# Eight recurrent heads of one encoder layer: the head outputs made with tokens on the partitions, their squares summed along the free axis, scaled, and turned around by PE

## The reference, cut to what matters

```
o  = (q * exp(G)) @ S_before_chunk  +  tril(att) @ v          # 128 numbers per token and head
o  = o * rsqrt(mean(o * o, over the 128 numbers) + eps) * a_gnorm
o  = o * silu(og)
```

## Time and profile before

| | us |
|---|---|
| median of 3 runs | 2349.55 |
| lowest, highest | 2348.75, 2355.37 |
| span of the profiled execution | 2347.9 |
| PE busy / DVE / ACT / POOL | 2281.0 / 1565.2 / 1268.0 / 1337.0 |

### The profile page before, as it was taken

How to read it: one execution, slowest core, us unless ns; L and a number is a source line. 1 busy time by engine, 2 the same in 40 slices (tenths; PEclk the granted TensorE clock), 3 DMA queues, 4 the chain that set the end, 5 groups by cost and what they waited for, 6 DMA issues and landing times.

```text
span 2347.9 us, 54490 instructions
## 1 busy us (share of the span) xinstructions
PE 2281.0 (97%) x20432; PEld 1959.8 (83%) x20432; DVE 1565.2 (67%) x2618; ACT 1268.0 (54%) x2295; POOL 1337.0 (57%) x1019
## 2 busy tenths in 40 slices
PE   8899999999998999999999999999999999999998
PEld 6788888888887888888878888877888888888886
DVE  7877777635589777777882332389687767445755
ACT  6454555433576666666554334554555544334775
POOL 2787777767515555555555444305777778677120
PEclk9999999999999999999999999999999999999999
DMA  3123222443530111111111212330232222535202
GB/s 132 50 83 101 92 77 86 151 143 103 166 100 20 40 46 46 44 39 41 49 43 49 63 48 86 115 101 28 86 92 89 86 77 86 178 122 194 76 19 75
DMA packets 155236, 194.93 MB, mean 83 GB/s; under 512 B 13168, under 2 KB 102512, under 8 KB 155120
## 3 DMA queue, kind: packets, MB, share of 16 engines
q1 hardware_dynamic: 111920, 153.59, 20.7%
q10 hardware_dynamic: 43200, 39.83, 5.2%
HBM read 155.49 MB, written 37.88 MB: 82 GB/s over the span
## 4 chain that ended last, share of the span: by engine, by line
PE 65%; DVE 13%; POOL 7%; issue 6%; ACT 5%; DMA 3%; SPq 1%; ACTq 0%; POOLq 0%; DVEq 0%
PE bank L1068 17%; PE bank L1071 17%; PE bank L1070 17%; PE bank L1035 4%; PE bank L1037 4%; PE bank L1036 4%; POOL ring L929 4%; DMA ring<-weights 3%; POOL ring L933 2%; DVE hid L2201 2%; DVE hid L2355 1%; DVE ops L2256 1%; DVE ops L2365 1%; DVE ops L2209 1%; PE bank L1201 1%
## 5 line engine op out<-in xcount | busy, mean ns | idle before, releaser
L1068 PE MATMUL bank<-ops,ring 128*128 128x264 f16 x4112 | 1139.4, 277 | 20.2 <-DVE work L2402 6.3
L1070 PE MATMUL bank<-ops,ring 128*128 128x264 f16 x4112 | 1138.7, 277 | 0.0
L1071 PE MATMUL bank<-ops,ring 128*128 128x264 f16 x4112 | 1138.6, 277 | 0.0
L929 POOL TENSOR_TENSOR ring<-ring 128x512 f16<-128x512 f32 (+1 forms) x492 | 659.8, 1360 | 273.8 <-ACT ring L1401 273.8
L1401 ACT ACTIVATE ring<-ring 128x512 f16<-128x512 f32 (+1 forms) x492 | 286.7, 614 | 501.8 <-POOL ring L933 498.3
L1068 PEld LDWEIGHTS bank<-ops,ring 128*128 128x128 f16 x4112 | 404.4, 98 | 91.3 <-issue 9.8
L1071 PEld LDWEIGHTS bank<-ops,ring 128*128 128x128 f16 x4112 | 403.7, 98 | 61.7
L1070 PEld LDWEIGHTS bank<-ops,ring 128*128 128x128 f16 x4112 | 403.7, 98 | 60.3
L914 POOL TENSOR_TENSOR ring<-wtmp,ring 128x512 f16<-128x512 f32 x107 | 130.8, 1227 | 340.9 <-ACT ring L1342 340.3
L1035 PE MATMUL bank<-hid,ring 128*128 128x264 f16 x1068 | 294.9, 276 | 1.5 <-issue 1.3
L1037 PE MATMUL bank<-hid,ring 128*128 128x264 f16 x1068 | 294.8, 276 | 0.0
(11 more groups left out here) (227 smaller groups left out, 3626.5 us busy)
## 6 DMA issues: line engine op xcount, KB each, us to landing
ring<-weights SPq DMA_DIRECT2D x363, 256.0 KB, 2.7
ops<-spill SPq DMA_DIRECT2D x16, 1056.0 KB, 6.9
ring<-weights SPq DMA_DIRECT2D x120, 128.0 KB, 2.4
spill<-hid ACTq DMA_DIRECT2D x42, 264.0 KB, 2.9
spill<-hid ACTq DMA_DIRECT2D x20, 528.0 KB, 5.0
ops<-spill SPq DMA_DIRECT2D x8, 792.0 KB, 5.1
hid<-xT SPq DMA_DIRECT2D x8, 528.0 KB, 8.3
hid<-out_x ACTq DMA_DIRECT2D x8, 528.0 KB, 7.3
```

The costliest lines, as they stand in the source:

```text
L929: nc.gpsimd.tensor_tensor(low(slot, kh), weight_source(name, k, kh), high(slot, kh), ALU.subtract)\
L1068: nc.tensor.matmul(out, whi, xhi, start=(kk == 0 and fresh(name, k)), stop=False, skip_group_check=True)
L1070: nc.tensor.matmul(out, whi, xlo, start=False, stop=False, skip_group_check=True)
L1071: mm = nc.tensor.matmul(out, wlo, xhi, start=False, stop=end, skip_group_check=True)
```

## The change

`head_outputs` swaps the operands: att or the decayed q (`W[5]`) is now the stationary side, v or the state `Sn` streams, and the output has tokens on partitions. `head_sumsq` goes. ACT squares the pieces (four of 256 columns and one of 64x128), DVE sums them with `tensor_reduce` into `osum` [128 x 9]. At the next turn ACT does Ln and Exp on `osum` (`orstd`), ahead of `logf`, and after `logf` copies the nine output tiles out of PSUM, each with its per-partition scale (`orows`). PE turns the nine tiles around (`output_transposes`, pieces OT), and DVE multiplies them, out of PSUM, with a_gnorm and silu(og) (`onorm`, which is now three instructions). The head loop of PE is written out for h = 1 and h = 8.

```diff
 HG_PIECES = (["vT"] * 3 + ["kT"] * 3 + ["L32"] * 2 + ["L16"] * 2 + ["D16"] * 2
-             + ["P"] * 5 + ["O"] * 4 + ["SS"] * 3)
+             + ["P"] * 5 + ["OT"] * 3 + ["O"] * 4)
+HG_LAST = (["vT"] * 3 + ["OT"] * 3 + ["kT"] * 3 + ["L32"] * 2 + ["L16"] * 2 + ["D16"] * 2
+           + ["P"] * 5 + ["O"] * 4)
-O_PAIRS = [(0, 3), (3, 6), (6, 8), (8, 9)]
+O_PAIRS = [(0, 2), (2, 4), (4, 6), (6, 9)]
...
# PE: head_outputs
-                            nc.tensor.matmul(bank[b][:, (j - j0) * P:(j - j0) * P + w], vtok[0:w, j * P:(j + 1) * P],
-                                             att[0:w, j * P:j * P + w],
+                            nc.tensor.matmul(bank[b][0:w, (j - j0) * P:(j - j0 + 1) * P], att[0:w, j * P:j * P + w],
+                                             vtok[0:w, j * P:(j + 1) * P],
...
-                            last = nc.tensor.matmul(bank[b][:, n * C:(n + 1) * C],
-                                                    Sn(c - 1 if c < PT else S_IN), W[5][:, c * C:(c + 1) * C],
+                            last = nc.tensor.matmul(bank[b][h0:h0 + C, n * P:(n + 1) * P],
+                                                    W[5][:, c * C:(c + 1) * C], Sn(c - 1 if c < PT else S_IN),
...
-            def head_sumsq(head):
-                pe.wait_ge(osq_ready, head * len(O_PAIRS) + len(O_PAIRS))
-                for r in range(3):
-                    c0, c1 = r * 512, min(r * 512 + 512, TP)
-                    def fill(b, c0=c0, c1=c1):
-                        return nc.tensor.matmul(bank[b][:, 0:c1 - c0], ones, osq[:, c0:c1], start=True, stop=True)
+            def output_transposes(turn_head, head):
+                for r in range(len(O_PAIRS)):
+                    b, uses = plan.piece(head, "O", r)
+                    pe.wait_ge(bank_read[b], uses + 1)
+                for r, (j0, j1) in enumerate(TOK_TILES):
...
+                            last = nc.tensor.transpose(bank[b][:, (j - j0) * P:(j - j0) * P + w],
+                                                       orow(head, j)[0:w, :], ident[0:w, 0:w])
...
# PE: hooks; `norms` is output_transposes(hh, hh - 1)
                     (0, 1): [lambda: values(h), lambda: head_transposes(hh, "vT", V)],
+                    (1, 1): norms if last else [],
...
                     (2, 1): [lambda: head_updates(hh, [4])],
+                    (3, 1): [] if last else norms,
                     (4, 1): [lambda: operands(hh, 8), lambda: head_outputs(hh)],
-                    (5, 1): [lambda: head_sumsq(hh)],
...
-            pair("gates", 0)
+            pair("gates", 0, None, {(1, 1): [lambda: output_transposes(HEADS, HEADS - 1)]})
...
# ACT
+            def orstd(head):
+                act.wait_ge(osum_ready, head * len(O_PAIRS) + len(O_PAIRS))
+                step(nc.scalar.activation(osum[:], osum[:], ACT.Ln, scale=1.0 / DK, bias=eps))
+                step(nc.scalar.activation(osum[:], osum[:], ACT.Exp, scale=-0.5))
+            def orows(head):
+                for r, (j0, j1) in enumerate(O_PAIRS):
...
+                        ins = nc.scalar.activation(orow(head, j)[0:w, :], bank[b][0:w, (j - j0) * P:(j - j0 + 1) * P],
+                                                   ACT.Copy, scale=osum[0:w, j:j + 1])
+                    ins.then_inc(bank_read[b], 1)
...
+                if with_norm:
+                    orstd(h - 2)
                 logf(hh)
                 state_load(hh)
...
-                    onorm(h - 2, RMS)
+                    orows(h - 2)
                 chain_copies("heads", p0, 0)
...
# DVE
+            def onorm(head, o):
...
+                    dve.wait_ge(bank_full[b], uses + 1)
+                    V_.scalar_tensor_tensor(out=o[:, t0:t1], in0=bank[b][:, 0:t1 - t0], scalar=anorm,
+                                            in1=og_of(head)[:, t0:t1], op0=ALU.mult, op1=ALU.mult)\
+                        .then_inc(bank_read[b], 1)
```

More of the change, by code:

```diff
@@ L624, in build, with orow @@
         U = [K_, Q, u1[:, :], V]
[L626 to L630, removed]
+        osq = ktok
+        R0 = area[:, 10 * TP + 18 * P + TP:10 * TP + 18 * P + TP + 512]
+        def orow(head, j):
+            if j == 8:
+                return work[0:C, 18 * P + 4 * N:19 * P + 4 * N]
+            if isinstance(head, int) and head == HEADS - 1:
+                return W[1][:, j * P:(j + 1) * P]
+            return R0[:, j * P:(j + 1) * P] if j < 4 else u1[:, TP // 2 + (j - 4) * P:TP // 2 + (j - 3) * P]
         UP, US = POOL_BUF, POOL_BUF + SEQ + POOL_BUF
@@ L1144, in calls, with piece @@
                 return [lambda c=c: norm(c) for c in cs]
-            def piece(head, n, fill):
-                b, uses = plan.piece(head, n)
+            def piece(head, kind, r, fill):
+                b, uses = plan.piece(head, kind, r)
                 take(b, uses)
@@ L1159, in fill @@
                         return last
-                    piece(head, HG_FIRST[kind] + r, fill)
+                    piece(head, kind, r, fill)
             def head_scores(head, kind, kk, qq):
@@ L1184, in fill @@
                         return last
-                    piece(head, HG_FIRST["P"] + r, fill)
+                    piece(head, "P", r, fill)
             def head_outputs(head):
@@ new lines, in output_transposes, with fill @@
+            def output_transposes(turn_head, head):
[3 more added lines that the diff above has]
+                for r, (j0, j1) in enumerate(TOK_TILES):
+                    def fill(b, j0=j0, j1=j1):
+                        for j in range(j0, j1):
+                            w = min(P, TP - j * P)
+                            last = nc.tensor.transpose(bank[b][:, (j - j0) * P:(j - j0) * P + w],
+                                                       orow(head, j)[0:w, :], ident[0:w, 0:w])
+                        return last
+                    piece(turn_head, "OT", r, fill)
@@ L1231, in head_hooks @@
                 hh = h - 1
+                first, last = (isinstance(h, int) and h == n for n in (1, HEADS))
+                norms = [] if first else [lambda: output_transposes(hh, hh - 1)]
                 return [{
                     (0, 1): [lambda: values(h), lambda: head_transposes(hh, "vT", V)],
+                    (1, 1): norms if last else [],
                     (2, 1): [lambda: operands(hh, 1), lambda: head_transposes(hh, "kT", W[3])],
@@ L1735, in wait_piece @@
             def wait_piece(head, kind, r):
-                b, uses = plan.piece(head, HG_FIRST[kind] + r)
+                b, uses = plan.piece(head, kind, r)
                 act.wait_ge(bank_full[b], uses + 1)
@@ L1793, in onorm_high @@
             def onorm_high(head, o):
-                act.wait_ge(o_scaled, head + 1)
+                for r in range(len(TOK_TILES)):
+                    b, uses = plan.piece(head + 1, "OT", r)
+                    act.wait_ge(bank_read[b], uses + 1)
                 nc.scalar.activation(split_of(head)[:, :, 0:N], o[:, 0:T].rearrange("p (g n) -> p g n", g=G), ACT.Copy)\
@@ L2776, in head_turn @@
                 if u_turn:
-                    dve.wait_ge(o_scaled, HEADS - 1)
+                    for r in range(len(TOK_TILES)):
+                        b, uses = plan.piece(hh, "OT", r)
+                        dve.wait_ge(bank_read[b], uses + 1)
                 sums_b_odd("heads", p0, b0)
@@ L2825, in outputs @@
                         onorm_low(h - 2, W[0])
[L2826 to L2835 removed]
+                    output_sums(hh)
                 if u_turn:
```

104 lines of the change are left out of this document (51 added, 53 removed).

## The result

The changed kernel takes 2374.26 us (median of 4 runs, 2370.33 to 2376.8) against 2350.25 for the kernel before on the same chip: ratio 1.0096, 95% interval 1.008 to 1.0111. It is slower by about 24 us, or 1%. The profiled execution, the fastest of the four, took 2370.33 us, with a span of 2368.2 at a mean clock of 0.988; before, the span was 2347.9 at 0.993, so it grew by 20.3. The forecast was 2371.

A forecast was written before the change was run, and what follows sets the result against it. PE (97% busy) and a path over ACT and DVE were taken to arrive level at vT, so PE's savings become waits. 3.9 + 2.8 + 12 + 4.0 = 22.7 us on the span of 2347.9 gave 2370.6, median 2371, range 2356 to 2380.

The forecast's parts named there:

- The level point: From product 4 to vT, PE's path and the ACT and DVE path are level within 0.2 us; PE savings become waits.
- Outputs: PE's 32 output instructions with the state overlap at 0.06 us each: 1.5 us less per turn, turned into wait at vT.
- The wait: PE's wait at the vT transposes grows from 0.17 to 3.9 us; 2.4 with serial outputs.
- Clock: The wait at vT lowers PE's clock: 2.0 us per turn, bounds 0 to 2.6, in turns 2 to 7, 12 us.
- the first rival, clock up: The longer wait at vT leaves PE's clock up: +9 us, 2359; chance 16%.
- Transposes: The nine output transposes stand ahead of product 4 in turns 2 to 7: 0.65 us per turn net, 3.9 us.
- ACT ahead of `logf`: A fifth square, Ln and Exp delay `logf`: net 0.4 us per turn, bounds 0.1 to 0.65; 2.8 us over seven turns.
- The reduces: DVE's reduces are hidden by ACT's sigmoids; if one of 256 columns cost over 0.5 us, up to 0.3 per turn.
- Last turn: kT waits for banks that DVE's norm frees, and the slip stays into the gates: net +4.0 us, bounds -1 to +5.
- The four terms: Transposes 3.9, ACT ahead of `logf` 2.8, clock 12 and last turn 4.0 us, summing to 22.7 us on the span.
- the releaser: Sign: PE's waits at the vT transposes in turns 2 to 8 are ended by DVE's sum or the scan.
- faster by slack on ACT: The ACT and DVE path shortens by more than 0.65 us per turn: 2343; chance 7%, together with a level outcome.

The follow-up runs named there:

- e7: The kernel before, with PE's sums of squares made by one cheaper bfloat16 pass: 2352.48 us, ratio 1.0002.
- e4: The changed kernel with PE's outputs in two blocks, all instructions with att, then all with the state: 2373.29 us, ratio 1.0094.
- e1: The changed kernel with ten unread f32 matmuls in product 0 of turns 2 to 8, filling PE's wait: 2365.64 us, ratio 1.0058.
- e2: The changed kernel with ACT's Ln and Exp of the nine sums behind `logf` instead of ahead: 2367.78 us, ratio 1.0065.
- e3: The changed kernel with ACT's squares of the outputs one pair of weights earlier: 2358.4 us, ratio 1.0027.
- e8: e3 with three of the nine output transposes per head, so not computing what was asked: 2353.38 us, ratio 1.0012.
- e9: e3 with DVE's norm of the last turn ahead of the two subtractions of reference columns: 2354.09 us, ratio 1.001.
- e10: The changed kernel with the edits of e2, e3, e4 and e9 together: 2348.02 us, ratio 0.9987.
- e5: e3 with the last turn's output transposes and DVE's norm behind those of kT: 2358.94 us, ratio 1.004.

## Why the prediction was right

**The level point.** That the saving on PE would become a wait was right, and e7 and e4 show it from both sides: 1 us taken off PE in the kernel before, 1.24 us in the changed one, and the time the same.

**Outputs: the term mis-sized.** I said 32 x 0.047 = 1.5 us less; it was 5.81 - 5.37 = 0.44. The instructions themselves are as priced from the score block: in e4 the 32 take 1.90 us, 0.059 each, where I took 0.06. What I had put at 0.1 us, a guess that no row supported, and left out of the sum, was the change of tiling. By e4 it costs some 0.17 us, and there are eight per head; the two products without a partner are the rest. The Trainium skill says in "TensorEngine Tiling (Array Packing)", section Tiling Modes, Key Properties, that changing the mode drains the engine. The trace agrees as far as each change costs time; a drain by itself no run here shows. As predicted, the term was worth nothing in the time.

**The wait** was to be 3.9 us and is 2.5: 1.06 less for the outputs, 0.2 less for ACT, and 0.1 that I have not traced.

**Clock: right in kind, too large.** I took six drops at 2.0 us in turns 2 to 7, 12 us, and 1.5 more in the last turn's term. There are six, at 1.65 (e1, and e2's own two turns), in turns 3 to 8. Five of them lengthen a turn, 8.3 us; the one in turn 8 is taken back by the kT wait (e3). No drop followed the kT wait in the changed kernel. My "near 0.94" for the clock was a slip: 3.4 us of 58 at half are 0.97, and 0.97 is what the window shows. The reasoning was weaker than the hit: a wait of 3.9 is far above what was harmless before, but the real one of 2.5 lies between 1.8 and 2.6, where no row of before decided. That it fell on the right side was luck. With waits 0.9 shorter (e3) the first rival, clock up, would have been true.

**Transposes: right.** From vT to the outputs the path grew by (894.60 - 852.97) - (890.89 - 851.46) = 2.20 us, 1.65 of it clock: 0.55, where I had 0.65. e8 shows it on the path.

**ACT ahead of `logf`: half.** `logf` starts 11.56 us behind the outputs' start instead of 11.02, 0.54 later: Ln and Exp take 906.16 - 905.45 = 0.71 and the squares 0.1 more, but 0.28 of it falls where `logf` waited for DVE before. The scan follows `logf` 1.23 us behind its start instead of 1.60, which gives back 0.37. Net 0.2 instead of 0.4. The reduces (0.42 us each at 256 columns) and the scaled copies (0.25 each, 2.4 together) were hidden, as said.

**Last turn: right, and the gates at nothing.** I had 4.0 us. Up to the first product of the gates it is 57.5 - 54.1 = 3.4, by the mechanism named, kT waiting for DVE's norm. The wait was 1.9 us and not 3.5, because PE arrives later itself, at low clock; when the clock is up it is 3.44 (e3). e9 takes the term away with one move. In the gates another 45.0 - 42.2 = 2.7 us came on top, which the sum did not have. I had said that PE's wait for DVE at the gates' product 3 would still be there and keep the slip; it is gone, and PE waits 1.92 us for ACT's scaled copies ahead of the last head's transposes instead.

So the sum, 3.9 + 2.8 + 12 + 4.0 = 22.7, was in truth about 3.3 + 1.2 + 8.3 + 3.4, and 2.7 in the gates: 18.9, against 20.3 of span. Of the 1.4 us left, half lies in the two stretches up to vT of turn 3 (51.92 and 56.48 us, 51.36 and 55.42 before), where no drop is; the other half in the turns behind the one I worked on, where the changed kernel's are up to 0.2 us longer and before's up to 0.3 shorter than that pair, for no reason that I found. The four terms were too large by 6.5 us together, 3.7 of it the clock's, and 4.1 us were missing: that the forecast of 2370.6 came so near the span of 2368.2 is partly luck.

Of the signs, the releaser, the wait ahead of product 4 that went, and the lowered clock came true. The wait at vT (2.2 to 2.7 us, not near 4), the block of outputs (5.37 us, not 4.2 to 4.9), the wait inside kT (1.94, not 3 to 4) and the wait at the gates' product 3 did not.

The rival "faster by slack on ACT" had the lever right (the squares' turn with POOL): the change does not pull it, and e3 does.

## What to carry to other kernels

Where two paths arrive level, work taken off the busy engine turns into an idle gap, and the gap can have a price of its own: here 2.5 us idle brought 1.65 us of lowered clock. So when an engine is relieved, shorten the other path by as much in the same change, here by one moved call; and if that can't be done, filling the gap can pay: work that nobody needs was worth 9 us here. Even with all repairs (e10) the change gains nothing that can be told from noise.
After a change that takes more banks, look at which instruction gives them back and move that one, not the one that waits: moving the waiting one (e5) only moved the wait.

## What the hardware showed that I had not expected

- The length of the wait alone does not tell whether the clock falls. Of the five vT waits of 1.96 to 2.15 us in e2, four were followed by 1.2 GHz; of the five of 1.99 to 2.16 us in e10, none. A wait of 3.4 us inside kT brought no low stretch in e3, 3.4 us of it in e2 and 6.8 in e1; one of 1.92 us in the gates of the changed kernel brought one, one of 2.20 us at the same place in e3 none. In e2 the instructions on both sides of the gap are the same in each of the five turns, so they alone do not decide it either. What does, no run here shows.
- A change between full tiles and 64-column tiles cost PE some 0.17 us (e4). In a block by themselves the instructions with 64 stationary columns, whose products go to alternate halves of the partitions, overlap in pairs: 0.059 us each for 128 streamed f32 columns, where the swapped form took 0.107.
- Ln on 9 columns took ACT 0.30 us and Exp 0.21; the Exp that needs the Ln started 0.03 us behind it, `logf` 0.17 behind the Exp.
